# Second banded attention: where the softmax is divided by its sums, and who copies the turned probabilities

## The chip, the cores and the metric

One NeuronCore of a Trainium2 chip runs the whole program as one launch. The metric is the device time of that launch in microseconds; the times shown are medians of runs, and one execution was profiled.

## The reference, cut to what matters

Two transformer blocks follow each other on a sequence of 1024 tokens and width 1024. The second block has a windowed attention with 8 query heads, 2 key heads, head width 64, a window of 128 tokens on both sides, 256 context keys and one sink logit per head. Each query block of 128 tokens sees its own key block, the one before and the one after (where there is one) and both context key blocks: 4 or 5 key blocks of 128.

```python
s_loc = einsum('bnqkgd,bnjkd->bnkgqj', qb, kb) * scale      # masked to the band
s_ctx = einsum('bnqkgd,bjkd->bnkgqj', qb, k_ctx) * scale
p = softmax(concatenate([sink, s_ctx, s_loc], axis=-1), axis=-1)
out = einsum('bnkgqj,bjkd->bnqkgd', p_ctx, v_ctx) + einsum('bnkgqj,bnjkd->bnqkgd', p_loc, vb)
x = x + gt1 * (concatenate([att, conv], axis=-1) @ w_out)
```

After it come the output projection, a router and 16 experts. All matrices are fp32; most products are made in two parts (a high fp32r part and a low rest) with three passes.

## The kernel before, in words

Each engine has its own program, and semaphores order them. The sequence is cut into NT = 8 query blocks n. A block n has two groups of four heads; the kernel counts these as b = 2n and 2n + 1 (here "block b", 16 of them), and single heads as units u = 4b + c (64 of them). For a unit, TensorE writes scores into one of two bank pairs (`att_scores`, lines 1257 and 1258), VectorE adds the mask, writes the result to SBUF and takes the negated maximum (`att_max`, line 2583), ScalarE takes the exponential in place and the sum beside it (`att_exp`, line 1912). VectorE then inverts that sum and multiplies the row by the inverse (`att_normalised`, lines 2590 and 2592). When the four units of a block are done, TensorE turns each of its key blocks (`att_turn`, line 1269, four 128x128 transposes into bank 4 or 5), ScalarE copies the bank to one of eight SBUF places (`att_turned_out`, line 1920), and TensorE multiplies values by it (`att_values`, line 1280: two matrix products of 64 output rows, one for each head group, each in two passes of 512 columns). The outputs of query block n are summed in bank 6 or 7, by turns; ScalarE copies them as a high part (`att_high`, line 1925) and VectorE stores the low rest (`att_low`, line 2597).

TensorE's order is written by hand. In block b it goes through the key blocks j: turn j, the scores of a unit of the next block (three of them, and one more after the last j), and value products that are due by the table `VALUES_AFTER`. Turn (b, 0) waits until all four units of block b are ready (`s_pn` in the kernel before). Score u waits for the maximum of unit u - 2, whose banks it takes. ScalarE goes through copy j, then the exponential of unit j of the next block. VectorE goes unit by unit. GpSimd writes the sink columns, and splits the queries of later blocks (lines 3002 and 3005) and the convolution's output (line 2993); SyncE moves the split queries.

Before block 0, TensorE makes the last input projection with the scores of units 0 to 3 between its passes, and VectorE finishes the gated convolution (line 2636). Block 0 also has the split of the queries of n = 1 on VectorE (`staged_low`, line 2571). Block 15 has no scores left to make; its turns and values lie between the products of the first two parts of the output projection (`output_part2`, lines 1072 to 1074). After them, the adding of the first part to the residual (line 2656), its squares on ScalarE (line 1523), the next weight's high part (line 1700) and its low part on GpSimd (line 2926) come one after another, the first of them behind the last `att_low` on VectorE.

Of the kernel before, what the change touches and what calls it, by code (L numbers as in the profile page):

```python
# [56 lines left out]
def bass_two_blocks(nc, T):  # L57
# [3 lines left out]
    with ExitStack() as ctx:  # L61
# [24 lines left out]
        (q_low,) = split_views(("q_low", 24, [2, HALF]))  # L86
# [99 lines left out]
        att_turned = [view(kb, HALF) for kb in (44, 46, 76, 78, 144, 146, 28, 30)]  # L186
# [33 lines left out]
        rec = tiny[:, 278:282]  # L220
        vpad = tiny[:, 282:286]
# [69 lines left out]
        s_fd = sem("forget_sum_ready")  # L291
# [16 lines left out]
        s_pn = sem("probs_normalised")  # L308
# [8 lines left out]
        s_gr = sem("group_inverse_ready")  # L317
# [25 lines left out]
        s_cx = sem("context_proj")  # L343
        s_cxe = sem("context_evacuated")
# [134 lines left out]
        LATE_STEPS = {(2, 5): (1, 3), (3, 5): (0, 2, 4), (3, 4): (0, 1, 3)}  # L479

        def values_after():

            at = {}
            for n in range(NT):
                nb = len(key_blocks(n))
# [11 lines left out]
        def turned_places():  # L497

            place, freed, free, done = {}, {}, [(i, 0) for i in range(8)], 0
            for b in range(2 * NT):  # L500
                for j in range(len(key_blocks(b // 2))):
                    late = [f for f in free if f[0] >= 6]
                    early = [f for f in free if f[0] < 6]
                    took = late[0] if (b // 2, j) == (NT - 2, 4) and late else early[0] if b >= 2 * NT - 2 else free[0]
                    free.remove(took)
                    place[b, j], freed[b, j] = took
                    for n, i in VALUES_AFTER.get((b, j), ()):
                        done += 1
                        free += [(place[2 * n, i], done), (place[2 * n + 1, i], done)]
            return place, freed  # L510

        TURNED_PLACE, TURNED_FREED = turned_places()

# [38 lines left out]
        def _(sp):  # L552
# [145 lines left out]
            for g in range(KT):  # L698
                sp.wait_ge(s_wlo, 2 * (G_OUT2 + g) - 2)
                sp.dma_start(slot[(G_OUT2 + g) % 2], out2[:, g % (KT // 2), :]).then_inc(s_wl[(G_OUT2 + g) % 2], 16)  # L700
                if g == 1:
                    for n in range(2, NT):
                        sp.wait_ge(s_krc, 2 * (n - 1) + 1)
                        for g2 in range(2):
                            sp.dma_start(q_st[HEAD_ROWS[1 - g2], 1 - n % 2, 4 * g2:4 * g2 + 4, :].bitcast(F32),
                                         q_low[HEAD_ROWS[g2], n % 2, :].bitcast(F32).rearrange("p (a b) -> p a b", a=4)).then_inc(QUERIES_MOVED[n % 2], 16)
# [54 lines left out]
        def _(pe):  # L761
# [510 lines left out]
            def att_values(n, j):  # L1272

                nb, block = len(key_blocks(n)), key_blocks(n)[j]
                pe.wait_ge(s_pt, U_ATT2 + BLOCKS_AT[2 * n + 1] + j + 1)
                if j == 0 and n >= 2:
                    pe.wait_ge(s_o, U_ATT2 + n - 1)
                v = v2[:, block, :] if block is not None else vc[:, j - nb + 2, :]
                for g, rows in enumerate(HEAD_ROWS):
                    m = pe.matmul(ps[rows, 6 + n % 2, :], v[:, rows], att_turned[TURNED_PLACE[2 * n + g, j]], start=(j == 0), stop=(j == nb - 1))  # L1280
                m.then_inc(s_pv, 1)

# [21 lines left out]
            for b in range(2 * NT - 1):  # L1304
                nb = len(key_blocks(b // 2))
                for j in range(nb):
# [6 lines left out]
                    for n, i in VALUES_AFTER.get((b, j), ()):  # L1313
                        att_values(n, i)
            pe.wait_ge(s_max, U_ATT2 + 8 * NT)
# [3 lines left out]
            output_part2(0, {2: lambda: att_turn(b, 0), 4: lambda: att_turn(b, 1), 5: lambda: att_values(n, 0), 6: lambda: att_turn(b, 2), 7: lambda: att_values(n, 1)})  # L1319
            output_part2(1, {0: lambda: att_turn(b, 3), 1: lambda: att_values(n, 2), 3: lambda: att_values(n, 3)})  # L1320
# [187 lines left out]
        def _(act_e):  # L1508
# [394 lines left out]
            def att_exp(u):  # L1903
# [5 lines left out]
                if u >= 4:  # L1909
# [1259 lines left out]
```

## Time and profile before

| what | us |
|---|---|
| median of 3 runs (lowest, highest) | 2465.41 (2464.05, 2467.61) |
| profiled execution, its own time | 2462.14 |
| its span, first to last instruction | 2460.3 |
| TensorE busy in it | 2364.8 (96%) |
| VectorE, ScalarE, GpSimd busy | 1550.9, 1226.5, 775.2 |

The span leaves out 1.8 us of the execution around it. The stage of the change runs from about 1577 us (block 0) over 1704 us (block 15) to 1726 us (the third part of the output projection). Times in the rows are microseconds from the span's start; the time after it is how long the entry lasts, which for matrix products overlaps with the next one, so that the distance between two starts is what a step costs TensorE.

### The profile page before, as it was taken

The numbers are of one execution on the slowest core, as the hardware profiler recorded it, in microseconds if no ns is written. First come the engines' busy times: TensorE is split into PE (matmuls) and PEld (weight loads), VectorE is DVE, ScalarE is ACT, GpSimd is POOL, SyncE is SP. The second block draws the span as 40 slices with busy tenths as digits, with TensorE's granted clock in tenths as the row PEclk, the third lists the DMA queues.
The fourth block names the chain that finished last, engine by engine and source line by source line (L and its number), as shares of the span: only waits on it lengthen the run. The fifth ranks groups of instructions, "written<-read, shape, count | busy, mean of one in ns | idle before, by whom it ended". The sixth has DMA issues, their size and how long they took to land.

```text
span 2460.3 us, 31957 instructions
## 1 busy us (share of the span) xinstructions
PE 2364.8 (96%) x11318; PEld 1875.9 (76%) x11318; DVE 1550.9 (63%) x2249; ACT 1226.5 (50%) x1807; POOL 775.2 (32%) x422
## 2 busy tenths in 40 slices
PE   8999999999999999999999999899997999999996
PEld 6786777778888788877788778765764877888885
DVE  4224567746643357864532734686257999999998
ACT  4112654434443323443334411375246888888887
POOL 0311100123444585444565221241311123222210
PEclk9999999999999999999999999999998999999998
DMA  7210000032222362222233111000448999999996
GB/s 286 76 35 1 1 36 1 1 137 86 93 96 100 140 243 99 86 86 103 85 120 107 64 69 47 27 18 5 172 177 308 399 398 395 386 389 390 388 388 233
DMA packets 87563, 385.67 MB, mean 157 GB/s; under 512 B 8173, under 2 KB 9373, under 8 KB 72481
## 3 DMA queue, kind: packets, MB, share of 16 engines
q1 hardware_dynamic: 82704, 366.83, 39.6%
q0 software_dynamic: 4752, 17.43, 2.7%
q8 instruction: 66, 1.08, 0.2%
q14 instruction: 41, 0.33, 0.0%
HBM read 361.60 MB, written 21.05 MB: 156 GB/s over the span
## 4 chain that ended last, share of the span: by engine, by line
PE 48%; issue 11%; DVE 9%; POOL 4%; ACT 3%; DMA 1%; POOLq 0%; DVEq 0%; ACTq 0%; SPq 0%
PE ps L1072 10%; PE ps L1074 10%; PE ps L1073 9%; PE ps L1441 5%; PE ps L1443 5%; PE ps L1442 5%; POOL w_lo L2926 4%; DVE e_lo L2778 3%; DVE arena L2592 1%; DVE arena L2583 1%; PE ps L1269 1%; DMA arena<-in_w_gate 1%; ACT arena L1912 1%; PE ps L1348 1%; PE ps L1477 1%
## 5 line engine op out<-in xcount | busy, mean ns | idle before, releaser
L2926 POOL TENSOR_TENSOR w_lo<-arena,w_hi 128x1024 fp32r<-128x1024 f32 x188 | 457.1, 2432 | 698.4 <-ACT w_hi L1700 690.5
L2778 DVE TENSOR_TENSOR e_lo<-arena,e_hi 128x1024 fp32r<-128x1024 f32 x384 | 450.8, 1218 | 33.2 <-ACT e_hi L2029 28.8
L2029 ACT ACTIVATE e_hi<-arena 128x1024 fp32r<-128x1024 f32 x384 | 401.3, 1060 | 85.6 <-PE ps L1443 80.3
L1700 ACT ACTIVATE w_hi<-arena 128x1024 fp32r<-128x1024 f32 x188 | 198.4, 1055 | 366.8 <-PE ps L1074 366.7
L1072 PE MATMUL ps<-h_hi,w_hi 128*128 128x512 f32 x848 | 336.6, 397 | 8.2 <-POOL w_lo L2926 5.1
L1074 PE MATMUL ps<-h_hi,w_lo 128*128 128x512 f32 x848 | 331.9, 391 | 0.0
L1073 PE MATMUL ps<-h_lo,w_hi 128*128 128x512 f32 x848 | 331.6, 391 | 0.0
L1441 PE MATMUL ps<-e_hi,x_hi 128*128 128x512 f32 x512 | 204.5, 399 | 5.2 <-DVE e_lo L2778 3.0
L1443 PE MATMUL ps<-e_lo,x_hi 128*128 128x512 f32 x512 | 199.7, 390 | 0.0
L1442 PE MATMUL ps<-e_hi,x_lo 128*128 128x512 f32 x512 | 199.5, 390 | 0.0
L1072 PEld LDWEIGHTS ps<-h_hi,w_hi 128*128 128x128 f32 x848 | 160.1, 189 | 48.0 <-issue 12.1
L1074 PEld LDWEIGHTS ps<-h_hi,w_lo 128*128 128x128 f32 x848 | 160.1, 189 | 34.1
L1073 PEld LDWEIGHTS ps<-h_lo,w_hi 128*128 128x128 f32 x848 | 160.3, 189 | 33.5 <-issue 1.2
L2456 DVE SCALAR_TENSOR_TENSOR arena<-ps,cols,arena 128x511 f32<-128x511 f32 x88 | 63.8, 746 | 174.1 <-ACT arena L1788 174.0
L1072 PE MATMUL ps<-a_hi,w_hi 128*128 128x512 f32 x352 | 137.7, 391 | 2.1 <-POOL w_lo L2926 2.0
L2125 DVE TENSOR_TENSOR arena<-arena 128x512 f32<-128x512 f32 (+2 forms) x85 | 92.8, 1092 | 74.0 <-ACT arena L1523 70.1
L1073 PE MATMUL ps<-act_lo,w_hi 128*128 (+1 forms) x352 | 137.0, 389 | 0.0
L1074 PE MATMUL ps<-a_hi,w_lo 128*128 128x512 f32 x352 | 136.9, 389 | 0.0
L1788 ACT ACTIVATE arena<-ps,cols 128x512 f32<-128x512 f32 x88 | 63.7, 774 | 140.6 <-PE ps L1074 139.0
L1441 PEld LDWEIGHTS ps<-e_hi,x_hi 128*128 128x128 f32 x512 | 96.1, 188 | 33.8 <-DVE e_lo L2778 9.8
L3064 POOL DMA_INDIRECT residual_rows<-arena,tiny x15 | 27.3, 1821 | 289.2 <-DVE arena L2785 251.2
L1443 PEld LDWEIGHTS ps<-e_lo,x_hi 128*128 128x128 f32 x512 | 96.1, 188 | 20.6
(399 smaller groups left out, 4951.9 us busy)
## 6 DMA issues: line engine op xcount, KB each, us to landing
arena<-in_w_up SPq DMA_DIRECT2D x108, 1024.0 KB, 8.5
arena<-in_w_down SPq DMA_DIRECT2D x86, 1024.0 KB, 8.4
arena<-in_w_gate SPq DMA_DIRECT2D x64, 1024.0 KB, 10.1
arena<-in_w_in SPq DMA_DIRECT2D x18, 1024.0 KB, 4.8
arena<-in_w_out SPq DMA_DIRECT2D x16, 1024.0 KB, 4.9
arena<-in_w_ada SPq DMA_DIRECT2D x12, 1024.0 KB, 10.6
arena<-in_w_ada SPq DMA_DIRECT2D x24, 512.0 KB, 6.7
routed_rows<-arena SPq DMA_DIRECT2D x8, 520.0 KB, 8.1
```

The source lines that it names most:

```text
L1072: pe.matmul(out, w_hi[:, q, w], hi, start=start, stop=False)
L1073: pe.matmul(out, w_hi[:, q, w], lo, start=False, stop=False)
L1074: return pe.matmul(out, w_lo[:, q, w], hi, start=False, stop=stop)
L1441: pe.matmul(out, hi[:, k, :], e_hi[:, r, w], start=(k == 0), stop=False)
L1442: pe.matmul(out, lo[:, k, :], e_hi[:, r, w], start=False, stop=False)
L1443: m = pe.matmul(out, hi[:, k, :], e_lo[:, r, w], start=False, stop=(k == KT - 1))
L1700: act_e.activation(w_hi[:, q, :], slot[c][:, q * D:(q + 1) * D], ACT.Copy).then_inc(s_whi, 1)
L2029: act_e.activation(e_hi[:, (2 * sl + a) % RING, :], slot[sl][:, a * D:(a + 1) * D], ACT.Copy).then_inc(s_ehi, 1)
L2125: v.tensor_tensor(sm[:, 0:n], sm[:, 0:n], sqs[k % 2][:, 0:n], ALU.add).then_inc(s_add, 1)
L2456: vc_.mark(v.scalar_tensor_tensor(convy[b][q][:, 1:HALF], ps[:, 2 * b + q, 0:HALF - 1], cols[:, bass.ds(t + w1, 1)], convy[b][q][:, 1:HALF ...
L2778: v.tensor_tensor(e_lo[:, r, :], slot[sl][:, a * D:(a + 1) * D], e_hi[:, r, :].bitcast(F32), ALU.subtract).then_inc(s_elo, 1)
L2926: gp.tensor_tensor(w_lo[:, q, :], slot[c][:, q * D:(q + 1) * D], w_hi[:, q, :].bitcast(F32), ALU.subtract).then_inc(s_wlo, 1)
```

## The change

The probabilities stay unscaled. VectorE no longer multiplies each row by an inverse; it inverts eight sums at once per query block (`att_inverses`). TensorE spreads these inverses over 64 rows each (`inverses_broadcast`: eight products of a broadcast column with the identity, 128 columns each, into bank 7), ScalarE copies them to SBUF (`att_inverses_out`), and VectorE multiplies the summed values by them (`att_scaled`) into `q2`, from which high and low part are taken. All values are now summed in bank 6, so the first values of n + 1 wait for `att_scaled(n)`. Turn (b, 0) waits for the exponentials. Of the turned banks, VectorE copies j = 1 and 3 and ScalarE the others. The value products are put into fewer places of TensorE's order. There are 12 places for turned banks, the last four over the staged queries, used in block 15. One buffer less holds the low parts of moved queries.

```diff
@@ values_after
-                steps = [(2 * n + 1, 1), (2 * n + 1, 2 if n == NT - 1 else 3)]
-                if n < NT - 1:
-                    steps += [(2 * n + 2, j) for j in LATE_STEPS[nb - 2, len(key_blocks(n + 1))]]
+                blocks = [(n, j) for j in range(len(key_blocks(n)))]
+                if n == NT - 1:
+                    at[2 * n + 1, 3] = blocks
                 else:
-                    steps += [(2 * n + 1, 3)] * 2
-                for j, step in enumerate(steps):
-                    at.setdefault(step, []).append((n, j))
+                    at[2 * n + 1, 2], at[2 * n + 2, 1], at[2 * n + 2, 3] = blocks[0:2], blocks[2:4], blocks[4:]
...
+        TURNED_BY_DVE = (1, 3)
+
+        def turned_copies(b, j):
+
+            every = [(c, i) for c in range(b + 1) for i in range(len(key_blocks(c // 2))) if (c, i) <= (b, j)]
+            dve = sum(i in TURNED_BY_DVE for c, i in every)
+            return (s_pn, dve) if j in TURNED_BY_DVE else (s_pt, U_ATT2 + len(every) - dve)
@@ TensorE
                 if j == 0:
-                    pe.wait_ge(s_pn, 4 * b + 4)
+                    pe.wait_ge(s_exp, U_ATT2 + 4 * b + 4)
                 if c >= 2:
-                    pe.wait_ge(s_pt, U_ATT2 + c - 1)
+                    pe.wait_ge(*turned_copies(*BLOCK_OF[c - 2]))
...
-                pe.wait_ge(s_pt, U_ATT2 + BLOCKS_AT[2 * n + 1] + j + 1)
-                if j == 0 and n >= 2:
-                    pe.wait_ge(s_o, U_ATT2 + n - 1)
+                pe.wait_ge(*turned_copies(2 * n + 1, j))
+                if j == 0 and n:
+                    pe.wait_ge(s_fd, 2 + n)
...
+            def inverses_broadcast(n):
+
+                pe.wait_ge(s_gr, 4 + n + 1)
+                if n:
+                    pe.wait_ge(s_cxe, 2 + n)
+                for c in range(4):
+                    for g, rows in enumerate(HEAD_ROWS):
+                        at = 8 * (n % 2) + 4 * g + c
+                        m = pe.matmul(ps[rows, 7, c * P:(c + 1) * P], att_rec[:, at:at + 1].to_broadcast([P, HD]), ident, start=True, stop=True)
+                m.then_inc(s_cx, 1)
...
+                    if b and b % 2 == 0 and j == 1:
+                        inverses_broadcast(b // 2 - 1)
...
-            output_part2(0, {2: lambda: att_turn(b, 0), 4: lambda: att_turn(b, 1), 5: lambda: att_values(n, 0), 6: lambda: att_turn(b, 2), 7: lambda: att_values(n, 1)})
-            output_part2(1, {0: lambda: att_turn(b, 3), 1: lambda: att_values(n, 2), 3: lambda: att_values(n, 3)})
+            output_part2(0, {1: lambda: att_turn(b, 0), 3: lambda: att_turn(b, 1), 4: lambda: att_turn(b, 2), 6: lambda: att_turn(b, 3),
+                             7: lambda: (inverses_broadcast(n), att_values(n, 0), att_values(n, 1))})
+            output_part2(1, {1: lambda: (att_values(n, 2), att_values(n, 3))})
@@ ScalarE
+            def att_inverses_out(n):
+
+                act_e.wait_ge(s_cx, 2 + n + 1)
+                act_e.wait_ge(*TURNED_FREED[n])
+                act_e.activation(att_turned[TURNED_PLACE[n]], ps[:, 7, :], ACT.Copy).then_inc(s_cxe, 1)
...
-                    att_turned_out(b, j)
+                    if j not in TURNED_BY_DVE:
+                        att_turned_out(b, j)
...
+                    if b and b % 2 == 0 and j == 2:
+                        att_inverses_out(b // 2 - 1)
@@ VectorE
-            def att_normalised(u):
-
-                b, c, w = u // 4, u % 4, band_keys(u // 8) + CTX
-                v.wait_ge(s_exp, U_ATT2 + u + 1)
-                vc_.link(v.reciprocal(rec[:, c:c + 1], den[:, c:c + 1]))
-                row = att_probs[b % 2][:, c, 0:w]
-                v.tensor_scalar(row, row, rec[:, c:c + 1], None, ALU.mult).then_inc(s_pn, 1)
+            def att_turned_out(b, j):
+
+                c = BLOCKS_AT[b] + j
+                v.wait_ge(s_T, U_ATT2 + c + 1)
+                if TURNED_FREED[b, j][1]:
+                    v.wait_ge(*TURNED_FREED[b, j])
+                v.tensor_copy(att_turned[TURNED_PLACE[b, j]], ps[:, 4 + c % 2, :]).then_inc(s_pn, 1)
+
+            def att_inverses(n):
+
+                v.wait_ge(s_exp, U_ATT2 + 8 * n + 8)
+                at = slice(8 * (n % 2), 8 * (n % 2) + 8)
+                v.reciprocal(att_rec[:, at], att_den[:, at]).then_inc(s_gr, 1)
+
+            def att_scaled(n):
+
+                v.wait_ge(s_pv, U_ATT2 + VALUES_DONE[n])
+                v.wait_ge(s_cxe, 2 + n + 1)
+                v.tensor_tensor(q2[:, :, n * P:(n + 1) * P], ps[:, 6, :].rearrange("p (a b) -> p a b", a=4),
+                                att_turned[TURNED_PLACE[n]].rearrange("p (a b) -> p a b", a=4), ALU.mult).then_inc(s_fd, 1)
...
-            for u in range(4, 8 * NT + 1):
-                if u % 4 == 0 and u > 4:
-                    att_normalised(u - 1)
-                if u < 8 * NT:
-                    att_max(u)
-                if u % 4:
-                    att_normalised(u - 1)
+            for u in range(4, 8 * NT):
+                att_max(u)
                 if u == 5:
                     staged_low(1)
-                if u % 8 == 2 and u >= 18:
+                if u % 8 == 0:
+                    att_inverses(u // 8 - 1)
+                if u % 8 == 0 and u >= 16:
+                    att_scaled(u // 8 - 2)
+                if u % 4 in TURNED_BY_DVE:
+                    att_turned_out(u // 4 - 1, u % 4)
+                if u % 8 == 3 and u >= 16:
                     att_low(u // 8 - 2)
-            for n in (NT - 2, NT - 1):
-                att_low(n)
+            att_inverses(NT - 1)
+            att_scaled(NT - 2)
+            att_turned_out(2 * NT - 1, 1)
+            att_low(NT - 2)
+            att_turned_out(2 * NT - 1, 3)
+            att_scaled(NT - 1)
+            att_low(NT - 1)
```

## Rows read from the trace of the kernel before

**Rows 1.** Windows: length, busy (count) of PE, PEld, DVE, ACT, POOL; PEclk; DMA.

```profile
1588.00:1594.00 6.00, 5.93 (x21) 4.13 (x21) 3.86 (x11) 2.81 (x6) 1.04 (x2) 0.51 0.15 34
1623.40:1640.13 16.73, 15.18 (x92) 10.13 (x92) 14.45 (x34) 12.45 (x27) 6.91 (x8) 1.00 0.07 17
```

**Rows 2.** Timeline of TensorE, blocks 7 and 8: start, length, line, operation, idle before.

```profile
1640.13 0.66 PE L1269 MATMUL ps<-const,arena 128*128 128x128 f32 x4 [1.10 <-DVE arena L2592]
1640.55 0.42 PE L1257 MATMUL ps<-k_h,q_st 128*128 128x384 f32 x1
...
1641.23 0.60 PE L1269 MATMUL ps<-const,arena 128*128 128x128 f32 x4
1641.59 0.42 PE L1257 MATMUL ps<-k_h,q_st 128*128 128x384 f32 x1
...
1642.36 1.08 PE L1280 MATMUL ps<-arena 128*64 128x512 f32 x4
1643.37 0.66 PE L1269 MATMUL ps<-const,arena 128*128 128x128 f32 x4
...
1647.68 0.66 PE L1269 MATMUL ps<-const,arena 128*128 128x128 f32 x4 [0.45 <-DVE arena L2592]
...
1656.87 0.66 PE L1269 MATMUL ps<-const,arena 128*128 128x128 f32 x4 [1.10 <-DVE arena L2592]
```

**Rows 3.** Groups by line, VectorE and ScalarE, 1640.13 to 1656.87: busy, mean ns.

```profile
L2583 DVE CUSTOM_DVE_ANT_0 arena<-ps,arena,tiny 128x640 f32<-128x640 f32 x9 | 7.9, 877 | 1.7 <-PE ps L1258 1.7
L2592 DVE TENSOR_SCALAR arena<-arena,tiny 128x640 f32<-128x640 f32 x8 | 6.4, 796 | 0.3
...
L2597 DVE TENSOR_TENSOR o_lo<-ps,o_hi 128x512 fp32r<-128x512 f32 x1 | 0.7, 683 | 0.0
...
L1912 ACT ACTIVATE arena<-arena,tiny 128x641 f32<-128x641 f32 x8 | 6.6, 826 | 0.0
```

**Rows 4.** Waits of TensorE, 1570 to 1725: sum, times, longest.

```profile
PE ps L1269 <- DVE arena L2592: 15.4, 16, 2.3
```

**Rows 5.** TensorE elsewhere: 128-column fp32 passes in a timeline; loads of line 1280.

```profile
1390.46 1.05 PE L779 MATMUL ps<-arena,const 128*128 128x128 f32 x8
1391.35 1.46 PE L1227 MATMUL ps<-arena 128*128 128x256 f32 x6
...
L1280 PEld LDWEIGHTS ps<-arena 128*64 128x64 f32 x20 | 1.0, 134 | 0.7 <-issue 0.2
```

**Rows 6.** Timeline, TensorE and VectorE in blocks 0 and 1.

```profile
1578.54 0.39 PE L1257 MATMUL ps<-k_h,q_st 128*128 128x256 f32 x1 [0.67 <-DVE tiny L2637]
...
1584.95 0.41 PE L1257 MATMUL ps<-k_h,q_st 128*128 128x384 f32 x1 [2.54 <-DVE tiny L2583]
...
1588.07 1.11 PE L1269 MATMUL ps<-const,arena 128*128 128x128 f32 x4 [2.30 <-DVE arena L2592]
...
1581.97 2.05 DVE L2571 TENSOR_TENSOR q_st<-arena,q_st 64x512 fp32r<-64x512 f32 x2
```

**Rows 7.** Timeline of TensorE: first turns of blocks 4 and 14.

```profile
1614.20 0.66 PE L1269 MATMUL ps<-const,arena 128*128 128x128 f32 x4 [1.20 <-DVE arena L2592]
...
1697.61 0.66 PE L1269 MATMUL ps<-const,arena 128*128 128x128 f32 x4 [0.32 <-DVE arena L2592]
```

**Rows 8.** Timeline, TensorE and VectorE from block 15 to the third part.

```profile
1704.26 0.50 PE L1072 MATMUL ps<-o_hi,w_hi 128*128 128x512 f32 x1
...
1707.14 0.65 PE L1269 MATMUL ps<-const,arena 128*128 128x128 f32 x4 [1.23 <-DVE arena L2592]
...
1720.73 0.40 PE L1072 MATMUL ps<-c_hi,w_hi 128*128 128x512 f32 x1
...
1721.42 0.40 PE L1072 MATMUL ps<-c_hi,w_hi 128*128 128x512 f32 x1
...
1726.18 0.47 PE L1072 MATMUL ps<-o_hi,w_hi 128*128 128x512 f32 x1 [2.53 <-issue]
...
1721.29 0.74 DVE L2656 SCALAR_TENSOR_TENSOR arena<-ps,tiny,arena 128x512 f32<-128x512 f32 x1
```

More of the change, by code:

```diff
@@ L185, in bass_two_blocks @@
         att_probs = [view3(kb, 4, 644) for kb in (32, 64)]
-        att_turned = [view(kb, HALF) for kb in (44, 46, 76, 78, 144, 146, 28, 30)]
+        att_turned = [view(kb, HALF) for kb in (44, 46, 76, 78, 144, 146, 28, 30, 192, 194, 196, 198)]
         tok = [view(kb, ROW) for kb in (144, 148.25, 152.5, 156.75)]
@@ L342, in bass_two_blocks @@
         s_cl = sem("context_loaded_or_next_queries_moved")
-        s_cx = sem("context_proj")
-        s_cxe = sem("context_evacuated")
+        s_cx = sem("context_proj_or_heads_inverses_broadcast")
+        s_cxe = sem("context_or_heads_inverses_evacuated")
         s_cv = sem("conv2_done")
@@ L497, in turned_places, with take @@
         def turned_places():
-            place, freed, free, done = {}, {}, [(i, 0) for i in range(8)], 0
+            place, freed, free, done = {}, {}, [(i, (s_pv, 0)) for i in range(8)], 0
+            def take(key, spots):
+                at = next(f for f in free if f[0] in spots)
+                free.remove(at)
+                place[key], freed[key] = at
             for b in range(2 * NT):
+                if b >= 3 and b % 2:
+                    free.append((place[b // 2 - 1], (s_fd, 2 + b // 2)))
                 for j in range(len(key_blocks(b // 2))):
[L502 to L506, printed above, removed]
+                    if b == 2 * NT - 1:
+                        place[b, j], freed[b, j] = 8 + j, (s_S, U_ATT2 + 8 * NT)
+                    elif (b, j) == (2 * NT - 4, 4):
+                        take((b, j), (6, 7))
+                    elif b >= 2 * NT - 4 and any(f[0] < 6 for f in free):
+                        take((b, j), range(6))
+                    else:
+                        take((b, j), range(8))
                     for n, i in VALUES_AFTER.get((b, j), ()):
                         done += 1
-                        free += [(place[2 * n, i], done), (place[2 * n + 1, i], done)]
+                        if n < NT - 1:
+                            free += [(place[2 * n + g, i], (s_pv, U_ATT2 + done)) for g in range(2)]
+                    if b and b % 2 == 0 and j == 1:
+                        take(b // 2 - 1, range(6) if b == 2 * NT - 2 else range(8))
+            take(NT - 1, range(6))
             return place, freed
         TURNED_PLACE, TURNED_FREED = turned_places()
+        TURNED_BY_DVE = (1, 3)
[3 more added lines that the diff above has]
+            return (s_pn, dve) if j in TURNED_BY_DVE else (s_pt, U_ATT2 + len(every) - dve)
+        BLOCK_OF = [(b, j) for b in range(2 * NT) for j in range(len(key_blocks(b // 2)))]
         def sw_keys(b):
@@ L1314, in _ @@
                         att_values(n, i)
+                    if b and b % 2 == 0 and j == 1:
+                        inverses_broadcast(b // 2 - 1)
             pe.wait_ge(s_max, U_ATT2 + 8 * NT)
@@ L1908, in att_exp @@
                     act_e.wait_ge(s_si, b + 1)
-                if u >= 4:
-                    act_e.wait_ge(s_pn, u - 3)
                 row = att_probs[b % 2][:, c, 0:w + 1]
-                act_e.activation(row, row, ACT.Exp, bias=nmax[:, c:c + 1], scale=-1.0, accum_out=den[:, c:c + 1]).then_inc(s_exp, 1)
+                act_e.activation(row, row, ACT.Exp, bias=att_nmax[:, u % 8:u % 8 + 1], scale=-1.0, accum_out=att_den[:, u % 16:u % 16 + 1]).then_inc(s_exp, 1)
             def att_turned_out(b, j):
@@ L3004, in query_staged @@
                 for g, rows in enumerate(HEAD_ROWS):
-                    gp.tensor_tensor(q_low[rows, n % 2, :].rearrange("p (a b) -> p a b", a=4), q2[rows, :, n * P:(n + 1) * P],
+                    gp.tensor_tensor(q_low[rows, :].rearrange("p (a b) -> p a b", a=4), q2[rows, :, n * P:(n + 1) * P],
                                      q_st[rows, 1 - n % 2, 4 * g:4 * g + 4, :].bitcast(F32), ALU.subtract).then_inc(s_krc, 1)
@@ L3022, in _ @@
                 elif b == 14:
-                    for n in (NT - 2, NT - 1):
-                        gp.wait_ge(QUERIES_MOVED[n % 2], queries_moved(n))
+                    gp.wait_ge(QUERIES_MOVED[(NT - 1) % 2], queries_moved(NT - 1))
                     weight_low(G_OUT2, G_OUT2 % 2, 0)
```

35 lines of the change are left out of this document (16 added, 19 removed).

## The prediction

> **What bounds the kernel now.** First the view by windows, for the stage: in a steady pair of blocks TensorE is busy 15.18 of 16.73 us and VectorE 14.45, both far above ScalarE and GpSimd [rows 1]. Two engines near full mean that either can set the pace; the waits decide. The list of TensorE's waits has one large entry: 16 times, once for each block, its first turn waits for VectorE's multiplication by the inverse, 15.4 us together [rows 4]. The timeline of a pair shows where: TensorE runs without a break until the first turn of a block, where it stands 0.45 us (block 8) and 1.10 us (blocks 7 and 9) [rows 2]. The groups by line say why VectorE is late: eight maxima of 0.88 us and eight multiplications with a mean of 0.80 us [rows 3]. So VectorE bounds the stage, but TensorE is only some 10% behind it. What the change can give is bounded by that distance, less what it adds to TensorE.
>
> **TensorE's prices, start to start** [rows 2]. A turn after scores 1641.59 - 1641.23 = 0.36; after values or a wait 1640.55 - 1640.13 = 0.42. The scores of a unit 1641.23 - 1640.55 = 0.68. Values of one key block 1643.37 - 1642.36 = 1.01. Going over to values costs 1642.36 - (1641.59 + 0.68) = 0.09.
>
> **The added broadcast.** It is 8 products in two passes each, 16 passes of 128 columns, half of them into rows 0 to 63 and half into the others. No row shows it. Full-width fp32 passes of 128 columns follow each other at (1391.35 - 1390.46) / 8 = 0.111 us [rows 5]. The values show that the two halves run beside each other: four passes of 512 columns take 1.01, or 0.505 for two at once; a quarter of the columns makes 0.126. So 8 steps cost between 8 x 0.111 = 0.89 and, if the halves took turns, 16 x 0.111 = 1.78. I take 8 x 0.126 = 1.0 and 0.1 to go over, 1.1, since values are the same shape of work and stand right in front of it.
>
> The loads of weights are hidden in that number: four loads of a mean of 0.134 [rows 5] lie in the 1.01 of the values. The Trainium skill, "TensorE: Matmul & The Clock Gate", Part 3, says that a load overlaps with running products only where their row groups differ; these halves differ in columns alone. The case's rows speak against it here, since values with exposed loads would take longer than their passes; the time by the rule is one of the rivals.
>
> **Steady pairs.** Removed from VectorE, per pair: 8 multiplications and 8 inversions. Added: 4 copies at 0.68 (line 2597 also reads a bank [rows 3]), one inversion, one scaling at 0.68. VectorE goes from 14.45 to about 14.45 - 6.4 - 1.3 + 5 x 0.68 = 10.2, so it no longer sets the pace by its sum. The copies' bounds are 0.6 and 0.8; both leave VectorE well below TensorE. ScalarE loses four copies and gains one. TensorE, with the new order of values:
>
> Odd block: turn, scores, turn, scores 2.08; turn, scores 1.04; two values 0.09 + 2.02; turn, turn, scores 0.42 + 0.36 + 0.68: 6.69. One wait stays: the third scores need the maximum of the second unit, and VectorE now does maximum, inversion and scaling in front of it: 0.2 + 0.8 + 0.1 + 0.6 + 0.9 = 2.6 after the block's start, against 2.44 on TensorE. I take 0.2, bounds 0 and 0.6. Sum 6.9.
>
> Even block: 2.08; two values 2.11; broadcast 1.1; turn, scores, turn 0.42 + 0.68 + 0.36; values 1.10; turn, scores 1.10: 8.95. Does its successor's first turn wait for the exponentials instead? From the end of the last unit's scores: 0.2, maximum 0.88 + 0.08, exponential 0.83 + 0.19, together 2.2, and TensorE has 0.36 + 1.10 + 1.10 = 2.56 to do meanwhile. ScalarE copies the spread inverses (0.6) in that time, which leaves nearly nothing: hidden, but close.
>
> A pair is 15.85 against 1656.87 - 1640.13 = 16.74. Blocks 4 to 13 took 1697.61 - 1614.20 = 83.4 [rows 7]; five pairs now take 79.25: **4.2 us less**.
>
> **The start, blocks 0 to 3.** Unit 4's scores at 1578.54 waited for the end of the convolution on VectorE [rows 6], in front of which a multiplication (0.8) goes: 1577.7. Then the chain on VectorE is two maxima, the split of queries, now the first copy, a maximum. The split began at 1581.97 and took 2.05; without a multiplication and its wait in front it begins near 1580, and without the GpSimd work that now ran beside it, it is nearer to 1.4. Copy 0.68, maximum 0.75: the scores of unit 8, which waited 2.54, start near 1582.8 and not at 1584.95; maximum and exponential of unit 7 end near 1584.5. Block 1 started at 1588.07, after a wait of 2.30: 3.6 earlier. Blocks 1 and 2 then ran at a granted clock of 0.51, the 1.2 GHz level, from 1588 to 1594 [rows 1], after 5 us with little work on TensorE; at full clock that work takes about half, so 2.7 us are in it. With TensorE's waits in block 0 halved I take it that the clock stays. The same page of the Trainium skill, Part 1, ties the level to how busy the array was just before, which points the same way. Block 1 then costs 6.3 (an odd block with one turn less), block 2 7.8 and a wait of 0.75 (no third group of values covers its exponentials: 2.2 against 1.45), block 3 6.9: block 4 starts at 1584.5 + 21.75 = 1606.2, not 1614.20: **8.0 less**.
>
> **Block 14** took 1704.26 - 1697.61 = 6.65. Now: 2.08 - 0.2 (narrower scores) + 2.11 + 1.1 + 0.42 + 0.58 + 0.36 + 1.10 = 7.55: **0.9 more**.
>
> **The end.** The wait of 1.23 at the first turn of block 15 goes [rows 8]: the exponentials are hidden behind values and products. The broadcast adds 1.1. The chain that ends in the third part at 1726.18 (2.53 idle) runs from the last values over high part, low part, the addition at 1721.29, squares, high and low weights. The last values stand two product steps earlier, 2 x (1721.42 - 1720.73) = 1.38; the scaling adds 0.68 and a hop. Fewer changes to values give 0.2. -1.23 + 1.1 - 1.38 + 0.75 - 0.2 = **1.0 less**.
>
> **At nothing:** the eight inverses in one instruction, the missing buffer of query parts (GpSimd waits for a move made a pair earlier), the changed waits for places (freed a block earlier), and one output bank instead of two: the scaling ends about 1.8 us into an odd block, the first values that need the bank come at 5.2 - 2.0 = 3.2. If that cover went, each pair would cost 1 us. The low part now reads two operands from SBUF; it falls where GpSimd is idle.
>
> **Sum.** 8.0 + 4.2 - 0.9 + 1.0 = 12.3 us. The profiled execution, 2462.14 with its 1.84 outside the span, becomes 2449.8. It lay 3.3 below the median of the runs, 2465.41, so the median after is 2453.1. Nothing behind absorbs it: all later transfers are issued behind this stage.
>
> **Rivals.**
> A. The clock falls in block 1 all the same. For: the idle time in block 0 is not gone, and the low clock after 1588 shows that it is near the limit. Against: no single wait over 1.2 us remains. 12.3 - 2.7 = 9.6: 2455.8.
> B. The pace of the pairs does not change, since another chain takes the place of the removed one; the candidate is exponential behind inverse copy on ScalarE at the end of even blocks, with 0.3 us to spare. 12.3 - 4.2 = 8.1: 2457.3.
> C. The loads of the broadcast are not hidden: 8 x (0.111 + 0.134) = 1.96 for it, 0.86 more, eight times: 12.3 - 6.9 = 5.4: 2460.0. For: its passes are a quarter as long as those of the values, so there is less to hide them behind. It is the case of the skill's rule above.
> D. A and C together: 2.7 left, 2462.7, no change. Also here: VectorE's multiplication was not what held TensorE, only the last of several. Against: [rows 4] names it 16 times out of 16.
> E. Slower: the broadcast runs pass by pass, each pair of halves ending before the next loads. With the 1.05 - 7 x 0.111 = 0.27 that one pass lasts [rows 5] and 0.134 for the load, 8 x 0.41 = 3.3, eight times 2.2 more: 12.3 - 17.6 = -5.3: 2470.7. It decides from a broadcast of 1.1 + 12.3 / 8 = 2.6 on. Against: nothing in the rows runs like that.
>
> **Chances.** Forecast 0.45 (its own range 2450 to 2455), A 0.21, B 0.10, C 0.07, D 0.10, E 0.07. A measurement here tells about 0.2%, 4.9 us, from no change. Forecast, A, B and most of C are faster: 0.81; D and the rest of C the same: 0.12; E 0.07. The range goes from 2448 (broadcast 0.89, no wait in odd blocks: 1.7 + 1.6 more, and the runs' spread) to 2463 (up to D).
>
> **What would show it.** No TensorE wait for line 2592's place at a block's start and TensorE busy without a break over pairs of 15.6 to 16.1 us; broadcasts with about 1.1 us from their start to the next turn; a granted clock near 1.00 after block 1 starts. Wrong if the pairs stay near 16.7, if block 1 starts after 1586, or if the broadcast takes 2 us.

## The result and the profile after

The changed kernel takes 2450.68 us (median of 4 runs, 2447.87 to 2452.09) against 2465.68 for the kernel before (4 runs, 2464.05 to 2467.61): 15.0 us less. The ratio estimated from these runs is 0.9935, with a 95% interval from 0.9922 to 0.9949, or 12.6 to 19.2 us less. The forecast was 2453.1, 12.3 less. The profiled execution took 2447.87, of which 2446.1 are the span; before it was 2462.14.

The two timelines, cut at the same pieces of work, show where the 14.3 us between the two profiled spans come from. A stretch begins with the first scores of unit 0, with a block's first turn, with the first product of output part 0 or with that of the third part.

| stretch | before | after | difference | forecast |
|---|---|---|---|---|
| up to the first scores | 1568.58 | 1567.17 | -1.41 | 0 |
| first scores to block 1 | 19.49 | 15.75 | -3.74 | -3.6 |
| blocks 1 to 3 | 26.13 | 21.17 | -4.96 | -4.4 |
| blocks 4 to 13 | 83.41 | 76.60 | -6.81 | -4.2 |
| block 14 | 6.65 | 7.19 | +0.54 | +0.9 |
| block 15 to the third part | 21.92 | 20.02 | -1.90 | -1.0 |
| third part to the end | 734.15 | 738.16 | +4.01 | 0 |

The stage itself gains 16.9 us, 4.6 more than forecast. Behind it 4.0 are lost again, and 1.4 are gained ahead of it, where the programs are the same.

The windows of the profile after hold block 1, a steady pair (blocks 5 and 6), the start of the third part, and four microseconds in the last expert (length, busy and count of PE, PEld, DVE, ACT and POOL, then the granted clock, the DMA share and GB/s):

```profile
1582.92:1589.09 6.17, 6.17 (x41) 4.65 (x41) 4.06 (x11) 5.37 (x11) 3.18 (x5) 1.00 0.19 43
1612.71:1628.13 15.42, 15.42 (x110) 11.24 (x109) 10.45 (x23) 11.20 (x25) 6.49 (x8) 1.00 0.08 18
1707.90:1711.30 3.40, 3.40 (x9) 2.65 (x10) 0.45 (x1) 0.49 (x1) 2.37 (x1) 0.54 0.02 7
2415.62:2419.62 4.00, 4.00 (x9) 3.14 (x10) 3.35 (x5) 3.23 (x7) 0.00 (x0) 0.50 1.01 384
```

Against [rows 1]: the pair is 15.42 long and TensorE is busy in all of it; VectorE has gone from 14.45 to 10.45 (10.2 was forecast) and is no longer near the limit. Block 1 runs at a clock of 1.00, where it was 0.51. The last two rows are for later: the clock is low there.

The waits of TensorE, 1565 to 1712 (sum, times, longest), where [rows 4] had 15.4 us in 16 waits for line 2592:

```profile
PE ps L1092 <- issue: 1.9, 1, 1.9
PE ps L1289 <- ACT arena L1944: 1.7, 3, 0.7
PE ps L1289 <- DVE arena L2634: 1.0, 1, 1.0
PE ps L1277 <- DVE tiny L2689: 0.5, 1, 0.5
PE ps L1277 <- DVE tiny L2625: 0.2, 1, 0.2
```

Five kinds of wait are left, all of them in blocks 0 to 2 or in front of the third part (the 1.9). No block from 4 on waits at its first turn.

The timeline of TensorE, odd block 5 and even block 6, answers to [rows 2]; left out are scores and some turns:

```profile
1612.71 0.60 PE L1289 MATMUL ps<-const,arena 128*128 128x128 f32 x4
...
1614.75 0.60 PE L1289 MATMUL ps<-const,arena 128*128 128x128 f32 x4
1615.32 0.44 PE L1277 MATMUL ps<-k_h,q_st 128*128 128x384 f32 x1
...
1616.11 1.94 PE L1300 MATMUL ps<-arena 128*64 128x512 f32 x8
1617.97 1.10 PE L1289 MATMUL ps<-const,arena 128*128 128x128 f32 x8
...
1621.67 1.94 PE L1300 MATMUL ps<-arena 128*64 128x512 f32 x8
1623.44 1.04 PE L1311 MATMUL ps<-const,tiny 128*64 128x128 f32 x16
1624.42 0.66 PE L1289 MATMUL ps<-const,arena 128*128 128x128 f32 x4
...
1626.03 1.08 PE L1300 MATMUL ps<-arena 128*64 128x512 f32 x4
1627.04 0.66 PE L1289 MATMUL ps<-const,arena 128*128 128x128 f32 x4
```

Read the starts: the spreading of the inverses (line 1311) costs 1624.42 - 1623.44 = 0.98. Two value products in a row take 1617.97 - 1616.11 = 1.86 in front of a turn and 1623.44 - 1621.67 = 1.77 in front of the spreading, where a lone one takes 1627.04 - 1626.03 = 1.01. The one wait forecast for odd blocks is there too, though no idle time is printed: the third scores start 1615.32 - 1614.75 = 0.57 after their turn and not 0.36. VectorE's maximum of the second unit, which they need, runs from 1614.38 for 0.88 us, to 1615.26.

### The profile page after: what moved, and what is told of

Same layout as the page of the kernel before. It is cut to its first block, busy times and chain, and to the rows that moved or that the text cites. A ratio compares the mean times of both kernels' runs of the same rounds, so it can differ in the third digit from the quotient of the medians.

```text
span 2446.1 us, 32088 instructions
## 1 busy us (share of the span) xinstructions
PE 2366.8 (97%) x11446; PEld 1885.5 (77%) x11446; DVE 1523.2 (62%) x2169; ACT 1216.0 (50%) x1783; POOL 773.8 (32%) x422
## 4 chain that ended last, share of the span: by engine, by line
PE 51%; issue 11%; DVE 6%; POOL 4%; ACT 2%; DMA 1%; SPq 0%; POOLq 0%; DVEq 0%; ACTq 0%
PE ps L1092 10%; PE ps L1094 10%; PE ps L1093 10%; PE ps L1475 5%; PE ps L1477 5%; PE ps L1476 5%; POOL w_lo L2984 4%; DVE e_lo L2836 2%; PE ps L1300 1%; PE ps L1289 1%; PE ps L1277 1%; PE ps L1278 1%; PE ps L1382 1%; PE ps L1511 1%; DMA arena<-in_w_gate 1%
## 6 DMA issues: line engine op xcount, KB each, us to landing
arena<-in_w_gate SPq DMA_DIRECT2D x64, 1024.0 KB, 10.2
```

## The experiments

Since runs of one kernel lie up to 12 us apart, each experiment is read first from the lengths of the stretches, which repeat. The columns are those of the table above, for one profiled execution each; the last is the median of the timed runs.

| kernel | first scores | to block 1 | 1 to 3 | 4 to 13 | 14 | 15 to third part | to the end | median (runs) |
|---|---|---|---|---|---|---|---|---|
| changed kernel | 1567.17 | 15.75 | 21.17 | 76.60 | 7.19 | 20.02 | 738.16 | 2450.68 (4) |
| the same again | 1571.67 | 15.73 | 21.13 | 76.67 | 7.20 | 20.04 | 738.30 | 2451.14 (6) |
| before, no scaling | 1568.74 | 15.62 | 20.47 | 74.01 | 6.60 | 20.46 | 738.57 | 2446.06 (4) |
| before, values grouped | 1572.50 | 19.50 | 26.38 | 88.43 | 6.35 | 21.91 | 735.41 | 2474.13 (7) |
| spreading twice | 1566.83 | 15.74 | 22.05 | 81.00 | 8.06 | 20.90 | 736.38 | 2454.82 (4) |
| all copies on ScalarE | 1567.12 | 15.61 | 23.39 | 80.25 | 7.23 | 20.49 | 734.37 | 2458.81 (10) |
| values apart | 1573.64 | 15.74 | 21.34 | 78.57 | 7.20 | 20.02 | 739.49 | 2456.24 (4) |
| split three times | 1567.02 | 21.13 | 22.87 | 76.67 | 7.20 | 20.04 | 737.86 | 2456.33 (4) |
| weight first | 1573.89 | 15.73 | 22.79 | 76.68 | 7.20 | 17.96 | 736.33 | 2446.65 (4) |
| start and end | 1568.91 | 15.13 | 20.75 | 76.66 | 7.20 | 17.57 | 733.60 | 2442.66 (6) |
| start and end again | 1573.60 | 15.14 | 20.75 | 76.67 | 7.19 | 17.55 | 734.02 | 2444.78 (6) |

**The multiplication alone.** The kernel before, without the inversions and the multiplications, and with nothing in their place, so that the outputs are not divided by the sums:

```diff
-                    pe.wait_ge(s_pn, 4 * b + 4)
+                    pe.wait_ge(s_exp, U_ATT2 + 4 * b + 4)
...
-                if u % 4:
-                    att_normalised(u - 1)
```

> The kernel before with the inverses and the multiplication of the probabilities left out and nothing put in their place (no spreading, no scaling of the values; the outputs are not divided by the sums): turns wait for the exponentials, the order of TensorE and all copies stay. Theory 1, VectorE's multiplication held TensorE and TensorE itself is the next bound: a pair of blocks takes what TensorE was busy in it before, 16.74 - 1.55 of waits = 15.2 us; blocks 4 to 13 give 7.7, the start some 7 to 8, the end 1.2 of its wait: 16 to 17 us less than before, about 2449. Rival, the multiplication was only the last of several that come at nearly the same time: the turns wait for the exponentials instead, the pair stays above 16.4, and the time is within 5 us of before.

Its windows over the length of one pair, and its waits of TensorE from block 1 to the output projection's first product:

```profile
1618.13:1633.05 14.92, 14.92 (x94) 10.13 (x92) 7.74 (x18) 12.42 (x29) 6.48 (x7) 1.00 0.08 18
```

```profile
PE ps L1270 <- ACT arena L1911: 1.3, 2, 1.1
```

With VectorE's work at 7.74 the pair falls to 14.92 and no steady block waits (the two waits are in front of blocks 1 and 2): VectorE's multiplication, with its inversion, was what held TensorE, and TensorE is the next bound, a little lower than the 15.2 expected. The stage takes 137.2 us, so all that the change puts in its place, less what its grouped values save, costs 140.7 - 137.2 = 3.5 us. The median is 20.6 us under that of before (ratio 0.9924, interval 0.9907 to 0.9940). The rival, several things coming at nearly the same time, falls.

**The order of the values alone.** The kernel before, with the changed places for the value products of all query blocks but the last:

```diff
-                steps = [(2 * n + 1, 1), (2 * n + 1, 2 if n == NT - 1 else 3)]
...
+                    steps = ([(2 * n + 1, 2)] * 2 + [(2 * n + 2, 1)] * 2 + [(2 * n + 2, 3)])[:nb]
```

> The kernel before with the changed kernel's places for the value products alone (two, two, one instead of one by one), for all query blocks but the last. Theory 1, VectorE sets the pace: TensorE's work of a pair falls by some 0.5 to 0.75 us (a second value product in a row costs 0.86 and not 1.01), but the pair stays at 16.7 us and the waits at the blocks' first turns grow by the same amount; the time is within 2 us of before, 2463.5 to 2467.5. Rival, TensorE's order gave the gain: pairs of 16.0 to 16.2 us, and 4 us or more less than before.

A pair of it by windows, and the first turns in its timeline of TensorE:

```profile
1645.70:1662.96 17.26, 14.73 (x92) 10.31 (x92) 14.07 (x34) 12.54 (x27) 6.76 (x8) 1.00 0.07 17
```

```profile
1645.70 0.66 PE L1268 MATMUL ps<-const,arena 128*128 128x128 f32 x4 [0.61 <-DVE arena L2591]
...
1654.40 0.66 PE L1268 MATMUL ps<-const,arena 128*128 128x128 f32 x4 [1.92 <-DVE arena L2591]
```

TensorE is busy 14.73 and no longer 15.18 of a pair, but it waits 0.61 + 1.92 = 2.53 and no longer 1.55, so the pair grows from 16.74 to 17.26. The expected "within 2 us of before" was a miss on the slow side: the median is 7.5 us longer, the ratio 1.0030 (interval 1.0019 to 1.0042). While TensorE makes two value products it makes no scores, and VectorE, which sets the pace, stands still. Its groups by line, maxima and inversions of this pair and then the inversions of the pair before, from 1640.13 to 1656.87:

```profile
L2582 DVE CUSTOM_DVE_ANT_0 arena<-ps,arena,tiny 128x640 f32<-128x640 f32 x9 | 7.9, 878 | 2.1 <-PE ps L1257 2.1
L2589 DVE RECIPROCAL tiny<-tiny 128x1 f32<-128x1 f32 x8 | 1.3, 161 | 0.8 <-ACT arena L1911 0.8
L2590 DVE RECIPROCAL tiny<-tiny 128x1 f32<-128x1 f32 x8 | 1.3, 159 | 0.3 <-ACT arena L1912 0.3
```

VectorE stands idle for 2.1 us before the maxima and 0.8 before the inversions, where it was 1.7 [rows 3] and 0.3. The stage is 5.0 us longer: 0.5 in each of four pairs, 1.5 in the pair of blocks 12 and 13, and 1.5 in block 6, where the granted clock was 0.57 from 1636 to 1640. So this part of the change is a gain only once VectorE has room.

**The price of the spreading.**

```diff
-                for c in range(4):
+                for c in [*range(4), *range(4)]:
```

> The changed kernel with each spreading of the inverses made twice in a row into the same bank. Theory 1, TensorE has no slack left and 16 passes more cost what they take: 8 steps of 0.109 = 0.87 for each of the eight query blocks, pairs of 15.42 + 0.87 = 16.29 us, 7.0 us more in all, about 2457.5. Rival a, the spreading lies beside a wait that would be there anyway: pairs stay within 0.2 of 15.42, the time at 2450.7. Rival b, the loads of the spread columns come out once the queue of loads runs dry: 8 x (0.109 + 0.134) = 1.9 for each, 15 us more.

The timeline of TensorE, the doubled spreading and the turn behind it:

```profile
1624.84 1.92 PE L1311 MATMUL ps<-const,tiny 128*64 128x128 f32 x32
1626.69 0.66 PE L1289 MATMUL ps<-const,arena 128*128 128x128 f32 x4
```

1626.69 - 1624.84 = 1.85, that is 0.87 more than 0.98. The stage is 147.75 - 140.73 = 7.02 longer, and 8 x 0.87 is 7.0: TensorE has no slack. The 16 added passes cost 0.87 / 8 = 0.109 for two, where a full-width pass alone takes 0.111 [rows 5]: the two halves run beside each other and the loads are hidden. The medians lie only 4.1 us apart; behind the stage this run's profile is 1.8 us shorter than the changed kernel's.

**Who copies.** All five turned banks of a block copied by ScalarE:

```diff
-        TURNED_BY_DVE = (1, 3)
+        TURNED_BY_DVE = ()
...
-            att_turned_out(2 * NT - 1, 1)
...
-            att_turned_out(2 * NT - 1, 3)
```

> The changed kernel with all five turned banks copied by ScalarE. Theory 1, the copies on VectorE only take load from ScalarE, and what matters is the last exponential of a block: with a copy of 0.5 to 0.6 in front of it the chain from the last scores to the next block's first turn grows from 2.2 to about 2.8 us against 2.56 of work on TensorE: waits of 0.3 to 0.8 at the first turns, pairs of 15.7 to 16.9; block 0 gains about 1.0, since no copy stands before a maximum on VectorE; the time 2452 to 2458. Rival, ScalarE has room for all of it (some 12.6 us of 15.4): pairs stay at 15.42 and only block 0 changes, 2449.7.

The length of a pair by windows, and the waits of TensorE from 1585 to 1693, behind the first turn of block 1 and up to the end of block 14:

```profile
1613.41:1629.55 16.14, 15.60 (x110) 11.24 (x108) 8.30 (x19) 12.79 (x29) 6.51 (x8) 1.00 0.07 17
```

```profile
PE ps L1289 <- ACT arena L1944: 5.2, 9, 1.2
```

The pair is 0.72 longer and the first turns wait for the exponentials (in a steady pair 0.47 us at the even block, 0.07 at the odd one), though ScalarE is busy only 12.79 of 16.14: not its sum but the copy in front of the last exponential decides. Without the two copies on VectorE the stage would lose 6.2 of its 16.9 us. The 1.0 expected in block 0 were 0.13 (15.61 for 15.74): there the copy of the fourth bank, which goes to ScalarE as well, stands in front of the last exponential just as well.

**The grouping in the changed kernel.** Values of query blocks 0 to 4 one by one:

```diff
-                    at[2 * n + 1, 2], at[2 * n + 2, 1], at[2 * n + 2, 3] = blocks[0:2], blocks[2:4], blocks[4:]
+                    steps = [(2 * n + 1, 2), (2 * n + 1, 3), (2 * n + 2, 1), (2 * n + 2, 2), (2 * n + 2, 3)]
...
+                        at.setdefault(step, []).append(block)
...
```

> The changed kernel with the value products of query blocks 0 to 4 in five places, one by one (after the third and fourth turn of the odd block, the second, third and fourth of the even one), the others as changed. Theory 1, the value products in a row save TensorE the going over from and to other work: the kernel with the sums left out took 14.92 a pair with single products, the changed one 15.42 with a spreading of 0.97 more, so the grouping is worth 0.97 + 14.92 - 15.42 = 0.47 a pair: pairs of 15.9 us in blocks 2 to 10, some 2.3 us more in all, without a wait at a block's first turn. Rival, the grouping is worth nothing (its order only keeps the sums' bank out of the way): 15.42 stays, or waits appear at the first values of a query block instead.

Three starts of its timeline of TensorE, the first turns of blocks 5 and 7 and a lone value product in front of a spreading:

```profile
1619.61 0.60 PE L1293 MATMUL ps<-const,arena 128*128 128x128 f32 x4
...
1628.84 1.08 PE L1304 MATMUL ps<-arena 128*64 128x512 f32 x4
1629.74 1.04 PE L1315 MATMUL ps<-const,tiny 128*64 128x128 f32 x16
...
1635.59 0.60 PE L1293 MATMUL ps<-const,arena 128*128 128x128 f32 x4
```

The pair is 1635.59 - 1619.61 = 15.98, 0.56 longer (0.47 expected), and no steady block waits. The stage is 2.1 longer. The median, 5.6 longer, says more than that only by what lies outside the stage.

**The clock at the start.** Two more rounds of VectorE's split in block 0 (the function then makes its two steps three times):

```diff
...
-                    staged_low(1)
+                    staged_low(1, 3)
```

> The changed kernel with VectorE's low part of the split queries in block 0 made three times over (2 x 1.4 us more on VectorE, between the maxima of units 5 and 6). Theory 1, the low clock of blocks 1 and 2 before came from TensorE's idle time in block 0 (6.5 us of waits before, 2.8 now): with 2.9 more the granted clock falls again to about 0.5 in block 1, block 1 starts 2.9 later and blocks 1 to 3 take some 2.7 us longer: 5.6 us more in all, about 2456. Rival, the clock of these blocks depends on something else: only the 2.9 us are lost, blocks 1 to 3 stay at 21.2, about 2453.6.

Windows across block 0 and block 1:

```profile
1580.00:1584.00 4.00, 0.00 (x0) 0.00 (x0) 3.92 (x4) 0.00 (x0) 3.79 (x4) 0.70 0.00 0
1584.00:1588.00 4.00, 2.19 (x8) 1.85 (x8) 3.78 (x7) 1.43 (x4) 1.98 (x2) 0.50 0.28 66
1588.00:1592.00 4.00, 3.94 (x18) 3.85 (x18) 2.55 (x6) 2.21 (x6) 1.17 (x2) 0.52 0.01 2
1592.00:1596.00 4.00, 4.00 (x25) 2.49 (x24) 2.16 (x5) 3.51 (x8) 0.19 (x1) 1.00 0.00 0
```

TensorE stands still, the granted clock goes to the 1.2 GHz level, and it stays there for some 4 us of full work; block 1 takes 7.87 and not 6.17. The other profiles agree that idle time in block 0 brings the low clock: the three kernels in which TensorE stood still there for 6.0 to 7.3 us (before, values grouped, and this one) all had it in block 1 (0.71 to 0.83 over the block), and of the nine executions with 2.2 to 2.8 us only one had. The sizes were off: the added idle time was 5.4 us and not 2.9, since the six steps of 64 rows took 6.78 us, 1.13 each with GpSimd busy beside them (3.79 of 4.00), where the two of the changed kernel took 0.70 each; the clock cost 1.7 and not 2.7.

**The end.** The third weight's high part ahead of the last values' high part on ScalarE:

```diff
             att_inverses_out(NT - 1)
+            output2_high(2)
             att_high(NT - 1)
...
```

> The changed kernel with the third weight's high part made on ScalarE before the last high part of the values, and not behind the squares. Theory 1, the third part of the output projection waits for the weight's low part at the end of a chain from the last values (scaling, high, low, addition, squares, high and low weight): the weight needs none of it, so the idle 1.9 us goes, and with it the low clock behind it (8 passes at 0.43 and not 0.23: 1.6 us): 3.5 us less from the last values to the fourth part, about 2447. Rival a, the idle time goes and the clock falls all the same: 1.9 less. Rival b, the next part's weight is late instead (its high part still stands behind the squares): less than 1 us.

Windows of it: the first 5.4 us of block 1, the last 9 us ahead of the third part (which starts at 1714.26), and its first 2.2 us:

```profile
1589.62:1595.00 5.38, 5.38 (x28) 4.95 (x30) 3.44 (x9) 3.36 (x7) 2.99 (x4) 0.68 0.21 49
...
1705.00:1714.00 9.00, 9.00 (x40) 5.46 (x37) 2.32 (x4) 2.32 (x3) 2.38 (x1) 1.00 0.15 20
1714.26:1716.50 2.24, 2.24 (x11) 1.88 (x10) 1.34 (x2) 1.26 (x2) 0.00 (x0) 1.00 0.90 369
```

The idle time is gone (20.02 to 17.96), and with it the low clock, which was 0.54 in the 3.4 us behind it: up to the first expert weight the stretch is 1.7 us shorter as well, 3.8 in all against 3.5 expected. The wait does not bring the low clock every time: of the nine profiles that have it (1.9 to 2.5 us), eight have the low clock behind it, and the one with the split made three times has 1.00 there. The first row is a surprise: in this execution the clock fell in block 1 (7.79 for 6.17), behind a block 0 of the same program with the same waits. The forecast's rival A is thus real, in one of five executions with that same block 0 (the changed kernel twice, the spreading twice, the values apart, and this one).

**A better version.** The weight first, as above; all four last values behind the last spreading; turned bank 1 of block 0 by ScalarE; the last value product of query block 0 after the fourth turn of block 2:

```diff
-                             7: lambda: (inverses_broadcast(n), att_values(n, 0), att_values(n, 1))})
-            output_part2(1, {1: lambda: (att_values(n, 2), att_values(n, 3))})
+                             7: lambda: (inverses_broadcast(n), *[att_values(n, j) for j in range(4)])})
+            output_part2(1)
...
+            return j in (1, 3) and (b, j) != (0, 1)
...
+                    at[2 * n + 1, 2], at[2 * n + 2, 1], at[2 * n + 2, 3] = blocks[0:2], blocks[2:4 if n else 3], blocks[4 if n else 3:]
...
```

> The changed kernel with four small changes: the earlier weight of the run before; the last four value products in one place, behind the last spreading; turned bank 1 of block 0 copied by ScalarE and not VectorE; the last value product of query block 0 after the fourth turn of block 2, over the wait for its exponentials. Theory 1: 3.5 at the end and 0.25 for one place less; 0.5 in block 0 (the last exponential follows 0.5 earlier); 0.5 in block 2 (0.73 of wait less 0.25 for one place more): 4.7 us less than the changed kernel, about 2446. Rival, the pieces hide in each other or the clock falls at another place: 2449 to 2451.

Its waits of TensorE, 1565 to 1735:

```profile
PE ps L1291 <- ACT arena L1946: 1.0, 2, 0.6
PE ps L1279 <- DVE tiny L2629: 0.7, 1, 0.7
PE ps L1279 <- DVE tiny L2693: 0.5, 1, 0.5
```

2.2 us of waits are left of 5.3. The stage is 3.4 us shorter (0.6 in block 0, 0.4 in blocks 1 to 3, 2.5 at the end) and 1.7 more are saved behind it at full clock. The ratio to before is 0.9911 (interval 0.9894 to 0.9927).

**Once more, both.**

> The changed kernel once more, unchanged, to tell what repeats. By theory 1 what TensorE's order sets repeats to the hundredth: pairs of 15.42, 0.97 for a spreading, the end from block 15 to the third part 20.02; what can differ is where the granted clock falls: block 1 (6.17 in the first profile, 7.79 with the same program up to there in the run with the earlier weight) and the stretch near 326 us, long before the change, which took 5 us more in three of ten profiles. The time 2447 to 2456, median near 2451.

> The kernel with the four small changes once more, on the same chip as the changed kernel in this call, since single runs of one kernel lie up to 8 us apart. Theory 1: its stage took 137.31 us against 140.73 and the idle time before the third part is gone, so it is 3.4 us faster in the stage and 1.6 behind it: a median 5 us under the changed kernel's. Rival: what it gains is smaller than the spread of the runs, and the medians lie within 2 us.

Every stretch of both stages repeats within 0.07 us. The medians lie 6.4 us apart; the ratios to before, 0.9939 (0.9922 to 0.9957) and 0.9921 (0.9899 to 0.9942), overlap: the stretches show the gain of the better version, the timed runs alone do not. Over both sets the changed kernel has a median of 2450.68 (10 runs, 2446.21 to 2455.45) and the better one 2442.95 (12 runs, 2441.07 to 2453.67).

## Why the prediction was right, and where its sizes were off

*What bounds the stage.* Shown: with the multiplication gone, and nothing else done, the waits go and the pair is what TensorE was busy in.

*The spreading.* 1.1 was taken and 0.98 measured, 0.87 for a second one in a row. Rivals C (1.96) and E (3.3) are out: the 32 passes of the doubled spreading took 1.85 us, and no load shows. The sentence of the Trainium skill that C went by ("TensorE: Matmul & The Clock Gate", Part 3), that a load overlaps with running products only where their row groups differ, does not hold here as it stands, since the halves differ in columns alone; the same part also lets a load that goes to a background weight buffer be pulled ahead, which would fit, but no run here tells the two ways apart.

*Steady pairs* were the term most mis-sized: 15.42 and not 15.85, 6.8 us less and not 4.2. The step that failed is the price of the values: "Values of one key block 1643.37 - 1642.36 = 1.01" holds for a lone one and includes the going over to the next work; the second in a row adds 0.76 to 0.85. The two doubles are 2.02 - 1.86 = 0.16 and 2.02 - 1.77 = 0.25 cheaper, the spreading is 0.12 cheaper, and some 0.10 more goes into turns and goings over: 0.43 in all, 2.2 for five pairs. The other 0.5 is a slip in the sum: it took five equal pairs from the 83.4, but the pair of blocks 12 and 13, with narrower scores in front of block 14, took 16.46 before and takes 14.92 now. The wait of 0.2 in odd blocks came as forecast (0.57 - 0.36 = 0.21). Rival B is out, but its place was the right one to look at: one more copy on ScalarE in front of the last exponential brings part of it back (16.14).

*The start* came out as worked out: block 1 3.74 us earlier after the first scores (3.6), the wait of block 2 0.73 (0.75), and the clock at 1.00. That the clock stays was right for this execution and the repeat, and is no property of the program: it fell in the run with the earlier weight, one of five with this block 0; that the forecast met one of the other four was luck, at odds near the 0.21 it gave rival A. The same page of the Trainium skill, Part 1, says that the activity is judged in windows that run freely and don't start with the kernel; two executions with the same idle time and different clocks agree with that.

*Block 14 and the end* were 0.4 and 0.9 better, again mostly by the values: in block 14 one double and the cheaper spreading make the 0.4; at the end, four lone ones lay between products before, each 1.01 and some 0.2 of slower passes around it, and now two doubles.

*"Nothing behind absorbs it"* holds as far as shown, though this pair of profiles loses 4.0 us behind the stage. 2.5 of them are lost in the last expert: from the eighth last to the last low part of the expert weights it takes 14.1 us before, and 16.6 after and in the repeat. The clock tells why. The last row of the first fence above is the four microseconds behind the last two waits of TensorE, 1.72 and 1.07 us, at 0.50; in the windows of before, the same four behind the same waits (1.72 and 1.08):

```profile
2432.65:2436.65 4.00, 4.00 (x18) 3.31 (x19) 3.48 (x6) 3.87 (x8) 0.00 (x0) 1.00 1.02 381
```

The same work is ahead of both, and only in one the clock falls: 9 products and not 18. A further 1.4 are lost over the first 48 of the 384 low parts of the expert weights, 0.8 of them from 1879.53 to 1913.00, where the clock is 0.95 and before has 1.00 for the same work. Neither is an effect of the change. These 48 parts take 80.2 to 83.3 us over the twelve profiled executions, 80.5 before, 81.9 after and 82.3 with no scaling. Seven of the twelve executions have the low clock in the last expert (0.50 to 0.57, and 15.5 to 16.6 us for the eight parts), among them both edits of the kernel before, "no scaling" and "values grouped"; the five others, at 1.00 and 14.1 us, are before, "spreading twice", "all copies on ScalarE" and both of the better version. "All copies on ScalarE", which has the change, takes 734.37 us from the third part to the end, where before takes 734.15. Why the clock falls in one execution and not in another was not settled.

So the total, 15.0 us by medians (14.3 between the two profiles) against 12.3, is a stage that gave 4.6 more than forecast, and clocks elsewhere that in the one profiled pair took 2.6 net. That it came within 3 us of the forecast is in part luck; the terms, stretch by stretch, are what was right.

## What to carry to other kernels

When the list of waits names one instruction at every step, take that instruction off the engine, and price what replaces it in full on the engine that becomes the bound: here 20.4 us of the stage went with the multiplication, 3.5 net came back with its replacement, and a second spreading cost all of its 0.87 each time. Price a repeated product from two in a row, not from one between other work, and regroup TensorE's work only after the engine that feeds on it has room; grouping alone made this kernel 0.3% slower. And when idle time of TensorE goes, look for a low granted clock right behind it, since it can be worth nearly as much again (1.9 us of idle time and 1.7 of low clock in front of and behind the third part).

## What the runs showed of the hardware

**A clock that falls by chance moves a run by a third of the change.** In 4 of the 12 profiled executions the window from 324 to 336 us, long before the change, has a granted clock of 0.57 to 0.61, in the other eight 1.00; the programs are the same there. The first scores of the second attention start at 1572.5 to 1573.9 us in those four and at 1566.8 to 1571.7 in the others. From the 13th to the 16th high part of the weights on ScalarE (200 to 515 us) it takes 318.9 to 319.0 us in those four and 313.9 to 314.0 in seven of the others, 5 us less. The four have a low clock, down to 0.72, between 224 and 254 us as well; the repeat of the changed kernel has that one (and 0.84 to 0.87 from 500 to 512) without the one behind 324, and took 316.7. The rows are of the changed kernel and of the one with values apart:

```profile
324.00:336.00 12.00, 11.09 (x76) 8.45 (x75) 7.83 (x21) 4.56 (x13) 0.00 (x0) 1.00 0.45 176
```

```profile
324.00:336.00 12.00, 11.69 (x53) 9.07 (x53) 4.22 (x13) 3.50 (x11) 0.00 (x0) 0.57 0.36 137
```

**VectorE beside GpSimd.** The low part of the values, with two operands in SBUF, took 0.68 us in the changed kernel, where GpSimd was idle. In the better version the weight's low part on GpSimd falls on it, in the timeline:

```profile
1702.14 2.40 POOL L2988 TENSOR_TENSOR w_lo<-arena,w_hi 128x1024 fp32r<-128x1024 f32 x1 [10.92 <-ACT w_hi L1736]
1702.62 2.46 DVE L2656 TENSOR_TENSOR o_lo<-arena,o_hi 128x512 fp32r<-128x512 f32 x1 [1.87 <-ACT o_hi L1965]
```

VectorE ends 0.54 us after GpSimd does, less than the 0.68 that it takes alone, so it got little done until then. The Trainium skill, "SBUF — State Buffer", section "SBUF: two separate sides", says of a VectorE operation with two inputs in SBUF and a GpSimd operation that reads SBUF that the one that starts first holds their shared ports for its whole length, and the other waits; the two rows agree. Here it cost nothing, as the weight no longer stands behind it; the same pair of engines was busy when the added splits of block 0 took 5.4 us and not 2.9, though that the ports were the cause there was not tested.
